# The first norm by columns in four units, and four adaLN units moved to the out projection

## The reference, cut to what matters

```python
def rms_norm(x, g):
    y = xf * lax.rsqrt(jnp.mean(xf * xf, axis=-1, keepdims=True) + EPS)
    return y * g
def modulate(x, g, shift, scale):
    return rms_norm(x, g) * (1 + scale) + shift
```

## Time and profile before

| what | value |
|---|---|
| runs | 1761.1 us median of 3 (1760.04 to 1762.46) |
| span of the profiled execution | 1759.0 us |
| PE busy | 1687.6 us (96%) |
| DVE, ACT, POOL busy | 1026.4, 643.8, 277.3 us |
| granted TensorE clock, mean | 0.991 |

### The profile page before, as it was taken

The page is one execution under the profiler, slowest core; times in us unless marked ns, Lnnn a source line. Parts: engine busy times, 40 slices in busy tenths (PEclk is TensorE's granted clock), DMA queues, the critical chain, the costliest instruction groups (busy, mean ns, idle before and its releaser), DMA issues.

```text
span 1759.0 us, 26977 instructions
## 1 busy us (share of the span) xinstructions
PE 1687.6 (96%) x10042; PEld 1353.9 (77%) x10042; DVE 1026.4 (58%) x1938; ACT 643.8 (37%) x1090; POOL 277.3 (16%) x394
## 2 busy tenths in 40 slices
PE   5998899999999999999999999998999999999998
PEld 2876566668898888888888878875678788888886
DVE  4656565764747777777785681166743744443445
ACT  3323555663321212222324343245643333332343
POOL 1414333330300000000000031046421300000000
PEclk9999999999999999999999999999999999999999
DMA  8589441275513343434343543372503433332243
GB/s 314 191 262 304 108 111 24 46 95 190 190 52 97 103 136 106 132 113 127 97 144 108 179 168 126 114 186 58 145 10 108 144 96 95 95 95 81 86 133 132
DMA packets 265528, 224.27 MB, mean 127 GB/s; under 512 B 75224, under 2 KB 226136, under 8 KB 265432
## 3 DMA queue, kind: packets, MB, share of 16 engines
q1 hardware_dynamic: 257370, 206.42, 39.8%
q0 software_dynamic: 6048, 14.87, 2.2%
q10 hardware_dynamic: 2016, 1.71, 0.4%
HBM read 193.71 MB, written 29.25 MB: 127 GB/s over the span
## 4 chain that ended last, share of the span: by engine, by line
PE 84%; DVE 5%; ACT 3%; DMA 3%; issue 2%; POOL 2%; SPq 1%; ACTq 0%; DVEq 0%
PE ps L1252 30%; PE ps L852 11%; PE ps L853 11%; PE ps L854 11%; PE ps L1047 5%; PE ps L1129 4%; PE ps L1092 4%; PE ps L1262 2%; PE ps L1084 1%; PE ps L909 1%; ACT arena L1558 1%; PE ps L1237 1%; PE ps L1236 1%; PE ps L1238 1%; PE ps L1099 1%
## 5 line engine op out<-in xcount | busy, mean ns | idle before, releaser
L852 PE MATMUL ps<-w_hi,act_hi 128*128 128x512 f32 (+2 forms) x952 | 369.3, 388 | 2.1 <-DVE arena L2154 1.0
L853 PE MATMUL ps<-w_lo,act_hi 128*128 128x512 f32 (+2 forms) x952 | 364.7, 383 | 0.0
L854 PE MATMUL ps<-w_hi,act_lo 128*128 128x512 f32 (+2 forms) x952 | 364.7, 383 | 0.0
L1751 DVE TENSOR_TENSOR w_lo<-w_raw,w_hi 128x2048 fp32r<-128x2048 f32 (+4 forms) x114 | 206.9, 1815 | 243.8 <-ACT w_hi L1401 243.0
L1252 PE MATMUL ps<-act_lo,w_hi 128*128 128x512 f32 (+1 forms) x912 | 277.8, 359 | 0.0
L1252 PE MATMUL ps<-act_hi,w_hi 128*128 128x512 f32 (+1 forms) x912 | 276.2, 357 | 0.0
L1252 PE MATMUL ps<-act_hi,w_lo 128*128 128x512 f32 (+1 forms) x912 | 274.3, 355 | 0.0
L1401 ACT ACTIVATE w_hi<-w_raw 128x2048 fp32r<-128x2048 f32 (+3 forms) x108 | 168.7, 1562 | 270.9 <-PE ps L854 234.5
L852 PEld LDWEIGHTS ps<-w_hi,act_hi 128*128 128x128 f32 x952 | 179.7, 189 | 42.2 <-issue 8.8
L854 PEld LDWEIGHTS ps<-w_hi,act_lo 128*128 128x128 f32 x952 | 179.5, 189 | 34.0
L853 PEld LDWEIGHTS ps<-w_lo,act_hi 128*128 128x128 f32 x952 | 179.8, 189 | 32.5
(11 more groups left out here) (129 smaller groups left out, 2011.2 us busy)
## 6 DMA issues: line engine op xcount, KB each, us to landing
arena<-in_ada_w SPq DMA_DIRECT2D x44, 1024.0 KB, 8.5
w_raw<-in_ffn_up SPq DMA_DIRECT2D x88, 512.0 KB, 5.3
w_raw<-in_ffn_down SPq DMA_DIRECT2D x88, 256.0 KB, 3.0
w_raw<-in_odd_w_in SPq DMA_DIRECT2D x20, 512.0 KB, 4.6
arena<-mods SPq DMA_DIRECT2D x16, 512.0 KB, 6.5
proj_odd<-arena POOLq DMA_DIRECT2D x26, 256.0 KB, 2.4
x_after_mix<-arena SPq DMA_DIRECT2D x10, 512.0 KB, 2.9
arena<-x_after_mix SPq DMA_DIRECT2D x10, 512.0 KB, 5.2
```

Of the source, the lines that this page charges most:

```text
L852: mm(out_, s_hi, m_hi, start=start, stop=False)
L853: mm(out_, s_hi, m_lo, start=False, stop=False)
L854: return mm(out_, s_lo, m_hi, start=False, stop=stop)
L1751: V.tensor_sub(out_, full, hi.bitcast(fp32)).then_inc(sem_, 1)
```

## The change

**Head.** x comes first: four latent tiles into buffers of their own, then the first weight unit, then the wide units, whose 512 columns are now 256 of the shift and 256 of the scale, so that a unit covers two chunks of 128 features; context tiles reuse the buffers of the first two once these are turned. DVE multiplies the rows by the root alone, PE turns them, ACT copies them to `x_turned`. Per unit, PE makes the 512 numbers, DVE copies them, PE turns them into columns by four narrow products (`wide_turn`), DVE adds bias and gain and modulates the turned rows with two numbers per partition (`modulated`), ACT and DVE split, and PE multiplies the unit's two chunks (`products`). Units 0 and 1 do latent rows first, context rows behind both; units 2 and 3 do all rows. All of chunk 0 is now in this stage. The constants' DMAs move from ACT's queue to SP's.

**adaLN units.** The places move by two units, the input projection keeps 12 of the 16, and units 12 to 15 run behind tiles 2 to 5 of the out projection's second weight unit. Unit 12 is loaded when the last heads are turned, 13 when the last output is split, 14 and 15 behind the evacuation of 12 and 13, into two buffers.

```diff
-        ADA_AT = {(1, 5): [0, 1], (2, 1): [2], (2, 3): [3], (2, 5): [4], (3, 1): [5], (3, 3): [6], (3, 5): [7],
-                  (4, 5): [8], (5, 2): [9], (5, 5): [10], (6, 2): [11], (6, 5): [12], (7, 5): [13], (6, 8): [14],
-                  (6, 11): [15]}
+        ADA_AT = {(2, 1): [0], (2, 3): [1], (2, 5): [2], (3, 1): [3], (3, 3): [4], (3, 5): [5],
+                  (4, 5): [6], (5, 2): [7], (5, 5): [8], (6, 2): [9], (6, 5): [10], (7, 5): [11]}
+        ADA_IN_OUT = {2: 12, 3: 13, 4: 14, 5: 15}
...
+            for t in range(LT):
+                first_rows(t)
+            k_unit(0, I["even_w_in"][0], 0, 4, 0, MLA_IN)
             wide_unit(0)
+            wide_unit(1)
+            for t in range(LT, NT):
+                sp.wait_ge(t_done, 2 * (t - LT) + 2)
+                first_rows(t)
+            wide_unit(2)
+            k_unit(1, I["even_w_in"][0], 4, 4, 0, MLA_IN)
+            sp.wait_ge(t_done, row_round(0) + 1)
+            wide_unit(3)
...
+                if layer == 0:
+                    sp.wait_ge(left_free, base("swa", "tt") + SWA.prep_end(SWA.pairs - 1))
+                    sp.wait_ge(right_free, base("swa", "tt") + SWA.prep_end(SWA.pairs - 1))
+                    out_unit(12)
                 sp.wait_ge(o_lo, OL0 + base(nm, "hd"))
+                if layer == 0:
+                    out_unit(13)
                 mod_loads(nm)
                 gain_loads(nm)
                 x_moves(nm, range(2))
+                if layer == 0:
+                    for i in (14, 15):
+                        sp.wait_ge(t_free, ada_round(0, ADA_FIRST + i - 2) + 1)
+                        out_unit(i)
...
+            def wide_turn(n):
+                r = row_round(n) + 1
+                pe.wait_ge(t_free, r)
+                for c in range(WIDE // P):
+                    last = mm(bank(6 + r % 2, 2, 2 * c), wide_row[:, c * P:(c + 1) * P], sel[:, :], start=True, stop=True)
+                last.then_inc(t_done, 1)
...
+                for t in latent:
+                    rows_turn(t)
+                wide_mm(0)
+                wide_turn(0)
+                products(0, latent, 1)
+                wide_mm(1)
+                wide_turn(1)
+                products(1, latent, 2)
+                for t in context:
+                    rows_turn(t)
+                products(0, context, 3)
+                products(1, context, 4)
+                for n in range(2, WIDES):
+                    wide_mm(n)
+                    wide_turn(n)
+                    products(n, latent, 2 * n + 1)
+                    products(n, context, 2 * n + 2)
...
+                for t in range(LT):
+                    normed(t)
+                split_lo(0, 0, 4 * MLA_IN)
+                for n in range(2):
+                    modulation_columns(n)
+                    modulated(n, 0, row_round(n) + 2)
+                    low(n, 0, n + 1)
...
+                for n in range(2, WIDES):
+                    modulation_columns(n)
+                    for v in range(2):
+                        modulated(n, v, row_round(n) + 2)
+                    for v in range(2):
+                        low(n, v, 2 * n + v + 1)
...
                     if n == 0:
                         modulation(name)
+                        if layer == 0:
+                            for i in ADA_IN_OUT.values():
+                                early_evac(i)
```

More of the change, by code:

```diff
@@ L921, in norm_turn, with first_norm_products, rows_turn, products @@
                     turn(r, r, [src[:, (4 * half + k) * P:(4 * half + k + 1) * P] for k in range(4)])
[L923 to L931, removed]
+            def first_norm_products():
+                def rows_turn(t):
+                    pe.wait_ge(h_ready, t + 1)
+                    if t == LT:
+                        pe.wait_ge(t_free, turn_round(t))
+                    for half in range(2):
+                        r = turn_round(t) + half
+                        turn(r, r, [x_first[t][:, (4 * half + k) * P:(4 * half + k + 1) * P] for k in range(4)])
+                def products(n, tiles, part):
+                    weights(n // 2)
+                    pe.wait_ge(first_lo, part)
+                    for t in tiles:
+                        rows = slice(t * P, (t + 1) * P)
+                        for j in range(FEAT_K):
+                            k, at = n * FEAT_K + j, (n % 2 * FEAT_K + j) * MLA_IN
+                            cols = slice(at, at + MLA_IN)
+                            last = three(bank(t, MLA_IN), act_hi[:, k, rows], act_lo[:, k, rows],
+                                         w_hi[:, n // 2, cols], w_lo[:, n // 2, cols], k == 0, k == KC - 1)
+                        if n % 2:
+                            last.then_inc(mm_done, 1)
+                latent, context = range(LT), range(LT, NT)
+                for t in latent:
[15 more added lines that the diff above has]
+                    products(n, context, 2 * n + 2)
             def turned(name, t):
@@ L997, in in_projection @@
                     for n in range(2):
-                        if ci == 0 and (n == 0 or layer):
+                        if ci == 0:
                             u += 1
@@ L1199, in out_projection, with after @@
                 weights(u + 1)
-                unit_mm((u + 1) % 2, tiles, 4, 512, (act_hi, act_lo), 4, False, True)
+                def after(b):
+                    if layer == 0 and b in ADA_IN_OUT:
+                        ada_mm(ADA_IN_OUT[b])
+                unit_mm((u + 1) % 2, tiles, 4, 512, (act_hi, act_lo), 4, False, True, after=after)
                 u += 2
@@ L1833, in first_norm, with normed, modulation_columns @@
-                split_lo(1, 1, 4 * MLA_IN)
+                def normed(t):
+                    dve.wait_ge(rs_x, t + 1)
+                    V.tensor_scalar(x_first[t], x_first[t], rsx[:, t:t + 1], None, ALU.mult).then_inc(h_ready, 1)
+                def modulation_columns(n):
+                    r = row_round(n)
+                    dve.wait_ge(t_done, r + 1)
+                    V.tensor_copy(wide_row, bank(6 + r % 2, WIDE)).then_inc(t_free, 1)
+                    dve.wait_ge(t_done, r + 2)
+                    m = first_mod[:, n, :, :, :]
+                    V.tensor_add(m.rearrange("p s j v -> p (s j v)"), bank(6 + (r + 1) % 2, 2 * WIDE // P),
+                                 first_bias[:, n, :]).then_inc(t_free, 1)
+                    dve.wait_ge(t_free, r + 2)
+                    own.inc(V.scalar_tensor_tensor(out=m[:, 1], in0=m[:, 1], scalar=1.0,
+                                                   in1=first_gain[:, n].to_broadcast([P, FEAT_K, 2]),
+                                                   op0=ALU.add, op1=ALU.mult))
+                    own.wait()
@@ new lines, in modulated @@
+                def modulated(n, v, turned):
+                    dve.wait_ge(t_free, turned)
+                    rows = (slice(0, LAT), slice(LAT, ROWS))[v]
+                    for j in range(FEAT_K):
+                        x = x_turned[:, n * FEAT_K + j, rows]
+                        last = V.tensor_scalar(x, x, first_mod[:, n, 1, j, v:v + 1], first_mod[:, n, 0, j, v:v + 1],
+                                               ALU.mult, ALU.add)
+                    last.then_inc(first_set, 1)
@@ new lines, in low @@
+                def low(n, v, part):
+                    dve.wait_ge(first_hi, part)
+                    rows = (slice(0, LAT), slice(LAT, ROWS))[v]
+                    chunks = slice(n * FEAT_K, (n + 1) * FEAT_K)
+                    minus_hi(act_lo[:, chunks, rows], x_turned[:, chunks, rows], act_hi[:, chunks, rows], first_lo)
+                for t in range(LT):
[5 more added lines that the diff above has]
+                    low(n, 0, n + 1)
```

276 lines of the change are left out of this document (135 added, 141 removed).

## The result

The changed kernel takes 1786.2 us (median of four runs, 1785.2 to 1788.0) beside 1761.8 for the one before: a ratio of 1.0146, 95% interval 1.0131 to 1.0161. Run again later, beside other variants, it took 1788.3, 1.0154 (1.0141 to 1.0167). The profiled execution has a span of 1784.1 against 1759.0. Forecast were 1780 and a range of 1767 to 1790.

A forecast was written before the change was run, and what follows sets the result against it. PE, busy 96% of the span, was taken as the bound. Head +18.7, input projection -10.1 and out projection +10.6 make +19.2 on a span of 1759.0, 1778.2, or 1780 as a median of runs; range 1767 to 1790.

The forecast's parts named there:

- The head: Start to chunk 0 complete: each unit's latency bare on PE four times, plus slow clock; 96.1 against 77.4, +18.7 us.
- Rival B: Head and out projection: the clock does not fall in the gaps; head +9, out +9, 1769 us; chance 0.16.
- 1.9 each: Behind each idle stretch of PE: 3.8 us at half clock rate, a loss of 1.9 us.
- The two modulation passes of 512: VectorE in each head unit: 0.53 us a pass, 1.05 for two.
- The input projection: After the head: 11.6 us saved as four adaLN units go, less 1.5 of new wait; -10.1, bounds -11.6 and -4.
- the hole that I counted as pure gain: Input projection: PE's 6.03 us wait before the fifteenth adaLN unit, 6.0 of the 9.8 us that goes there.
- The out projection: Four units return, +4.0 us; PE waits 5.2 for unit 14's load, slow clock 1.4; +10.6, bounds +4 and +14.
- The gains: Out projection: modulation rows and gains land some 3 us later than 413.9, at 417.0, behind unit 13's load.
- The loads: Head: no later unit's weights are late; units 0 to 3 land near 17, 23, 31, 39; x first costs only unit 0.
- Rival C: Moved transfers collide: attention's first loads decide, input projection saves 4; unit 14's load takes 8.5, out +14; 1790 us; chance 0.12.
- the -4: Input projection: the lower saving of the forecast's bounds, -11.6 and -4 us around -10.1.
- Rival D: Head: short per-unit hand-over; from 3.5 us a unit down not slower, at 3.0 near 1759; chance 0.07, faster 0.05.

The follow-up runs named there:

- the head alone: The new head with all sixteen adaLN units back in the input projection; 1783.1 us, ratio 1.0126 to the kernel before.
- the new order: The changed kernel with its head's instructions in another written order, next units' weight and narrow products ahead of input products; 1756.6 us, ratio 0.9974 to the kernel before.
- dummies: The changed kernel with unread 96-column products before each unit's input products, 14 in unit 0, 28 in the others; 1785.5 us, ratio 1.0135 to the kernel before.
- after: The changed kernel itself, as against the kernel before; 1786.2 us, ratio 1.0146, and 1788.3 us, ratio 1.0154, when run again.
- the move alone: The kernel before with its old head and only the four adaLN units moved to the out projection; 1766.4 us, ratio 1.0033.
- three units later: The changed kernel with three adaLN units moved from among the first q and kv halves to the second; 1782.5 us, ratio 1.0127 to the kernel before.
- the load later: The changed kernel with one 1 MiB load of out weights issued behind the first pair's head loads; 1781.0 us, ratio 1.0117 to the kernel before.
- the shorter dummies: The changed kernel with fewer unread products, 8 in unit 0 and 19 in the others; median 1779.6 us, ratio 1.0115 to the kernel before.

## Why the prediction held, and where it did not

**The head**, +18.7 forecast, +19.3 measured. The mechanism is shown twice: the head alone costs 20.7, and another order of the same instructions takes 27.0 back. (Six kernels with this head have it done at 95.5 to 97.9, so the tenths mean little.) The terms were less exact than the sum. Unit 0's copy stood at 24.46 (forecast 22.9, as the identity came at 11.1 and held the first turns). From there to the products at 30.19 it took 5.7, 6.7 forecast; in units 1 to 3 the way from the last product to the next ones took 7.7, 8.3 forecast, and the context's 5.4, 5.6 forecast: together 2.8 short. The products behind the five stretches took 6.5, 6.2, 7.2, 8.9 and 9.0, which is 1.8 more than forecast. The start 1.6 late, the latencies 2.8 short and the products 1.8 dear nearly cancel; that is luck. Rival B fell with the windows at 0.50. Against products every 0.188 us the five falls cost 2.0, 1.7, 2.7, 2.1 and 2.2, not 1.9 each. That the clock falls anew in each round of a loop that waits in each round, there for a DMA, is what the Trainium skill says (TensorE: Matmul & The Clock Gate, HAM oscillation), and the trace agrees, where PE waits for VectorE; its cure, to keep the array fed, held here with real work (clock at 1.00 from 38 on in the new order, after 0.50 from 28 to 36 beside a PE that was mostly busy), not dependably with dummies.

The two modulation passes of 512 took 1.00 together in this row:

```profile
26.69 1.00 DVE L1931 TENSOR_SCALAR arena<-arena,first_mod 128x512 f32<-128x512 f32 x2
```

That is 0.50 each, and 0.75 for the scaling pass of 1024, so 512 elements more cost 0.25; of a tensor_tensor they cost 0.54 (0.68 for 512, 1.22 for 1024). This is the double rate of the Trainium skill (VectorE: DVE Perf Modes, the perf-mode tier table); the trace decides for it. I had 1.05.

**The input projection** is the step that failed: "I count 1.5 us of new wait: **-10.1**". It is 6.1 off, and so is the total, by the same 6. What PE no longer had to do was right: from chunk 0's end to attention's first turns (183.83, 7.2 later than before, 8 to 9 forecast) it took 87.4 us instead of 99.5. But attention's k came late by 4.5, its clock fell, and the stretch gained 4.0. The wait follows from a distance that I had not measured. In after, the last product of the first kv half stands at 172.03, and k is there at 189.17: 17.1 us for eviction, store, the wait for all stores, six q loads issued ahead of k, and the load. In the move alone it is 17.4 (151.94 to 169.36), with three units later 17.4 (169.20 to 186.61), with the load later 15.9. From that product to attention's first turns PE took 21.8 us in the kernel before (154.85 to 176.63), of it 6.0 the hole that I counted as pure gain; after, 11.8 are left. 17.1 less 11.8 and less the 0.8 of q turns is the wait of 4.5. My own numbers would have shown it: PE 9.8 us earlier, loads 5 to 6 earlier, is 4 of wait, not 1.5, if nothing was spare; I had assumed spare time without a row for it. The hole before the fifteenth unit had covered the k loads; with the head alone the hole is there, and PE waits for no k.

That makes 8.1 us lost between the first turns and the second pair's scores. The 3.6 beside the wait followed it, and the sum had no term for it: after's granted clock stood at 0.50 from 188 to 198 and again from 202 to 204, and from the first scores to the second pair's it took 10.6 us, 7.9 before.

**The out projection**, +10.6 forecast, +10.8 measured. Of it 9.6 lies behind tile 2 of the first weight unit (396.84 before, 413.34 after), and 1.2 within attention, where nothing was forecast and this profile has a wait of 1.17 for VectorE at 386.47; so here too errors cancel. Unit 14's load was issued at 438.54 and in by 443.85, 5.3 later, as forecast; PE waited 3.34 (5.2 forecast), at unit 15 not at all, as forecast. Where VectorE stood was right: its four passes began at 432.20 and the evacuation of unit 12 came behind them, 4.5 later. Taking just this order away gave 4.5 back. The gains let it start 1.8 later than before on the same scale (432.20 less 16.5, beside 413.91), where I had 3; that is most of the 1.9 by which the wait was shorter.

**The loads** of the head were no bound, as forecast: in the new order unit 3's product waited for none.

Rival C (attention's loads decide, unit 14's load takes 8.5) was half right: attention's loads decided, at the -4 that I had given as the end of the range; unit 14's load took 5.3. Rival D's condition, 3.5 us a unit or less, was not met in the written order. In the other order, where a unit's latency lies beside another unit's products, the head is 7.7 shorter than before and the kernel 0.3% faster.

## What to carry to other kernels

A step that is split into rounds of product, hand-over, hand-over, product costs its latency once a round unless the next round's first product and its hand-overs stand ahead of this round's long products in the written order; the same instructions made a head of 96 us or of 69. Before counting an idle stretch as gain, measure what else runs in it: here from the last producer of the next stage's data to the landed load. And on an engine that works in order, free the buffer that a load waits for before the long passes that nobody awaits yet.

## What the runs showed of the hardware

With dummies behind unit 1's narrow products PE was busy 1.19 us of 36 to 38 and all of 38 to 42, and the granted clock fell to 0.50 at 40 all the same (table above): work issued after the thin stretch came too late for that fall. Over the gap of unit 2 with 28 dummies and that of unit 3 with 19 it stayed at 1.00; in the other six gaps of the two profiles it fell. In the new order it fell once, and stayed at 0.50 from 28 to 36 while PE was busy 7.2 of the 8 us.

SyncE took 5.4 us to issue the six loads of q beside a full DMA, and 10.8 before the change; what is queued behind such loads starts later by that much.

In the six profiles with after's input projection and a k wait of 4.1 to 4.9 us, the first scores to the second pair's took 7.9 to 10.8 us. In the one of 7.9, that of the shorter dummies, the clock was at 1.00 from 194 on; in after it was at 0.50 until 198 and fell again at 202. A single profile of that stretch doesn't settle 3 us.
